# Where the operands of a split-fp32 matmul stream begin in SBUF: 256-byte buffer starts, and four buffers 4 to 28 bytes behind one

## Chip, cores, metric

One NeuronCore of a Trainium2 chip runs the whole program. The metric is the device time of one execution, in microseconds; the median of several runs counts.

## What is computed

A chain of transformer blocks over 512 tokens of 1024 channels, all in float32. `first_block` has two layers, each of a SwiGLU feed-forward, a mixer and a second feed-forward. `second_block` is one layer of two linear recurrences (gated delta rule and mLSTM), an output product, and a product-key expert layer over 16384 experts.

```python
x = x + 0.5 * swiglu(rmsnorm(x, ln_ffn1[l]), w_ffn1_gu[l], w_ffn1_down[l])
z = rmsnorm(x, ln_mix[l]) @ w_in[l]
a = pool_mixer(u_pool, ...) @ w_pool_branch[l]
b = swa_sink_attention(q, k, v, sinks[l]) @ w_attn_branch[l]
x = x + (g_pool * a + g_attn * b) @ w_out[l]
x = x + 0.5 * swiglu(rmsnorm(x, ln_ffn2[l]), w_ffn2_gu[l], w_ffn2_down[l])
...
x = x + concatenate([y_gdn, y_mlstm]) @ w_out_2
x = x + sum over chosen experts of gate * gelu(h . u_e) * v_e
```

## The kernel before

Activations lie transposed, 128 channels on the partitions and 512 tokens along the free dimension, so `x` is [128, 8, 512]. Every large product goes through weight tiles of [128, 2048] float32, 331 of them in all, one after the other through two slots. SP loads a tile into `raw`; ScalarE rounds it to float32r as `w_hi` (`split_hi`, L556); GpSimd writes the rest, `raw - w_hi`, as `w_lo` in four pieces (`low_part`, L448). The moving operand is split in the same way by ScalarE (hi) and VectorE (lo). A product of one 128x128 block is then three float32r matmuls of 512 columns into one PSUM bank (L1161 to L1163):

```python
pe.matmul(out_ap, w_hi[:, slot, cols], m_hi, start=start, stop=False)
pe.matmul(out_ap, w_hi[:, slot, cols], m_lo, start=False, stop=False)
return pe.matmul(out_ap, w_lo[:, slot, cols], m_hi, start=False, stop=stop)
```

The order of all work is written out by hand, engine by engine, with semaphores between them.

The moving operand is `h_hi`/`h_lo` in the gate and up columns, the input columns, the queries and the experts' first products; `act_hi`/`act_lo` ([128, 22, 512]) in the feed-forward's down product (`down`, L1248); `y` and `att` in the mixer's two branch products; `y` again and `mix_late` in its output product; `y2_hi`/`y2_lo` in the second mixer's output product, which the profile also calls y; and `w_mix_hi`/`w_mix_lo` ([128, 2, 4, 512]) in the experts' second products (`v_products`). `act_hi` is written by ScalarE at L590 and `act_lo` by VectorE at L2144; `w_mix_hi` by ScalarE at L1059 and `w_mix_lo` by VectorE at L2818. Groups of four expert rows alternate between two halves of the w_mix buffers.

`place` (L126) gives every buffer its address. It keeps a running offset that it rounds up to 32 bytes after each buffer, and adds `base`, the first free SBUF byte rounded up to 32, which is 16512 here. Buffers that all stages share come first (x, h, raw, w_hi, w_lo, rstd, sq, tmp, then small ones and constants); behind them, from `region`, each stage lays its own buffers over those of the others: the feed-forward, the mixer, the second mixer, the choice of experts, the experts.

Of the kernel before, what the change touches and what calls it, by code (L numbers as in the profile page):

```python
# [20 lines left out]
F32 = mybir.dt.float32  # L21
F32R = mybir.dt.float32r
# [5 lines left out]
P = 128  # L28
TOKENS = 512
# [4 lines left out]
FB = FF // P  # L34
# [8 lines left out]
GH = 4  # L43
# [16 lines left out]
EG = 4  # L60
# [53 lines left out]

GATE_STEP = {"rows": 1, "read": 2, "logs": 3, "a": 4, "sums": 5, "m": 7, "floor": 8}


def build(nc, x_in, weights, gains, small, pool_w, consts, rope, second, level_masks,
          keys, out):
# [2 lines left out]
    with stack:  # L122
        sizes = {F32: 4, F32R: 4, U32: 4}
        offset = [0]

        def place(name, shape, dtype, at=None):  # L126

            nbytes = int(np.prod(shape[1:])) * sizes[dtype]
            if at is None:
                at = offset[0]  # L130
                offset[0] = -(-(at + nbytes) // 32) * 32
            return nc.alloc_sbuf_tensor_at(name, shape, dtype, offset=at + base)

# [8 lines left out]


        x = place("x", [P, KB, TOKENS], F32)
        h_hi = place("h_hi", [P, KB, TOKENS], F32R)
        h_lo = place("h_lo", [P, KB, TOKENS], F32R)
        raw = place("raw", [P, 2, TILE * P], F32)
        w_hi_at = offset[0]
# [8 lines left out]
        rcol = place("rcol", [P, 3, TT], F32)  # L157
        gain = place("gain", [P, 9, KB], F32)
        small_sb = place("small_sb", [P, LAYERS, 14], F32)
        const = place("const", [P, 5, P], F32)  # L160
        mask = place("mask", [P, 2 * P], F32)
        invc = place("invc", [P, 4, PAD], F32)
        headsel = place("headsel", [P, 2], F32)
        rope_sb = place("rope_sb", [P, 2, TOKENS], F32)
        region = offset[0]
        ident, swap, upper, lower, ones = (const[:, n, :] for n in range(5))
# [1 line left out]

        offset[0] = region
        sq_ffn = place("sq_ffn", [P, KB, TOKENS], F32, at=region)  # L170
        act_hi = place("act_hi", [P, FB, TOKENS], F32R)
        act_lo = place("act_lo", [P, FB, TOKENS], F32R)
        gate_s = place("gate_s", [P, TOKENS], F32)
        up_s = place("up_s", [P, TOKENS], F32)
        silu = place("silu", [P, TOKENS], F32)
# [39 lines left out]
        head_gain = place("head_gain", [P, 8], F32)  # L215
        r3 = place("r3", [P, 3, TT, 8], F32)
        rn = place("rn", [P, 3, 32], F32)
        m_row_at = offset[0]
        m_row = place("m_row", [GH, 2, TOKENS], F32)
        head_squares = place("head_squares", [P, GH * P], F32, at=m_row_at)  # L220
        masks2 = place("masks2", [P, 9, P], F32)
        sq_second = place("sq_second", [P, KB, TOKENS], F32, at=offset[0])
# [75 lines left out]
        g_in = place("g_in", [P, 2, CHUNKS, EG, CHUNK], F32)  # L298
        sq_last = place("sq_last", [P, KB, TOKENS], F32, at=offset[0])
        s_in = place("s_in", [P, 2, EG, TOKENS], F32)  # L300
        w_mix_hi = place("w_mix_hi", [P, 2, EG, TOKENS], F32R)
        w_mix_lo = place("w_mix_lo", [P, 2, EG, TOKENS], F32R)
        gelu = place("gelu", [P, TOKENS], F32)
        weighed = place("weighed", [P, 2, TOKENS], F32)

# [2712 lines left out]
```

How the kernel before makes its waits and increments, by code:

```python
    def held(self):  # L89
        self.eng.wait_ge(self.sem, self.value())
# [253 lines left out]
        def wait_delta(eng, r, n):  # L345
            if delta_signals(r) == 7:
                if n < 7:
                    eng.wait_ge(sem("delta_done"), update_base[r] + n + 1)
                else:
                    eng.wait_ge(tile_used, update_end[r])
            elif n % 2 == 0:
                eng.wait_ge(sem("delta_done"), update_base[r] + n // 2 + 1)
            else:
                eng.wait_ge(tile_used, update_end[r] - 4 + n // 2 + 1)
# [64 lines left out]
        @block.sync  # L420
        def _(sp):
            sp.dma_start(raw[:, 0, :], weights[0]).then_inc(tile_landed[0], 16)
            for q in range(X_PARTS):
                sp.dma_start(x[:, 2 * q:2 * q + 2, :], x_in[:, 2 * q:2 * q + 2, :]).then_inc(x_landed[q], 16)
            sp.dma_start(raw[:, 1, :], weights[1]).then_inc(tile_landed[1], 16)
            with sp.Fori(0, (TILES - 2) // 2) as i:
                for slot in range(2):
                    source = sp.snap(2 * i + (2 + slot))
                    sp.wait_ge(lo_written, PIECES * (2 * i + (slot + 1)))
                    sp.dma_start(raw[:, slot, :], weights[source]).then_inc(tile_landed[slot], 16)
            sp.wait_ge(lo_written, PIECES * (TILES - 2))
            sp.dma_start(raw[:, 0, :], weights[TILES - 1]).then_inc(tile_landed[0], 16)
# [32 lines left out]
            def triangle(n, j):  # L466
                pool.wait_ge(sem("decay_exp"), pair_step(n, 1, j))
                e = q_mask[n % 2][j]
```

## Time and profile before

| what | value |
|---|---|
| median of 3 runs | 4127.03 us (4126.63 to 4129.42) |
| the profiled execution's own time | 4125.36 us |
| its span, first to last instruction | 4123.5 us |
| TensorE matmul busy | 4065.8 us, 99% of the span |
| weight loads (beside the matmuls) | 3366.7 us |
| VectorE, GpSimd, ScalarE busy | 1989.2, 1884.4, 1455.7 us |
| granted TensorE clock, mean | 0.997 of full speed |
| DMA | 489.64 MB, 119 GB/s mean |

A matmul's duration in the trace runs from its start until its result is in PSUM, and the next one starts before that; so durations of matmuls overlap, and how fast they follow each other is read from starts or from counts in a stretch. A granted clock of 1.00 is 2.4 GHz.

### The profile page before, as it was taken

Reading aid. Unit: us, or ns where it says so; the run is one execution under the profiler, and the core shown is the slowest. Engines: PE = TensorE matmul, PEld = TensorE weight load, DVE = VectorE, ACT = ScalarE, POOL = GpSimd, SP = SyncE. Lnnn points to the kernel's source line nnn. Section 1 sums busy time; section 2 is a strip of 40 time slices with the busy share of each in tenths; the row PEclk is TensorE's granted clock in tenths of the full one; section 3 lists DMA queues with packets and bytes.
Section 4 is the critical chain, followed back from the end, with each engine's and each line's share of the span. In section 5 each row is a group of like instructions: output and inputs, shape, how many; then the busy total and the mean of one; then the engine's idle time right before and its main releaser. Section 6 shows DMA issues by size and latency. Waiting matters only on the chain.

```text
span 4123.5 us, 52537 instructions
## 1 busy us (share of the span) xinstructions
PE 4065.8 (99%) x19252; PEld 3366.7 (82%) x19252; DVE 1989.2 (48%) x3472; ACT 1455.7 (35%) x2192; POOL 1884.4 (46%) x1408
## 2 busy tenths in 40 slices
PE   8999999999999999999999999999999999999998
PEld 7888777888888877888777998888888888888887
DVE  3212553221320354321148563498788846666653
ACT  3222243222322224322234433333677732222222
POOL 4444334444444434444432644455433345555553
PEclk9999999999999999999999999999999999999999
DMA  3222112222222222222322002233455575555542
GB/s 134 101 99 98 72 72 82 102 94 100 92 97 97 95 72 72 92 93 100 108 72 42 22 22 103 107 138 138 165 205 205 205 248 192 189 198 194 189 166 82
DMA packets 144611, 489.64 MB, mean 119 GB/s; under 512 B 17120, under 2 KB 82912, under 8 KB 101984
## 3 DMA queue, kind: packets, MB, share of 16 engines
q1 hardware_dynamic: 49392, 351.29, 24.2%
q10 hardware_dynamic: 95088, 136.56, 9.7%
q8 instruction: 86, 1.41, 0.1%
q14 instruction: 45, 0.37, 0.0%
HBM read 420.68 MB, written 67.14 MB: 118 GB/s over the span
## 4 chain that ended last, share of the span: by engine, by line
PE 42%; issue 33%; POOL 22%; DVE 2%; ACT 1%; POOLq 0%; ACTq 0%; DVEq 0%
POOL w_lo L448 21%; PE bank L1161 12%; PE bank L1162 12%; PE bank L1163 12%; PE bank L1974 1%; PE bank L1734 1%; PE bank L1750 1%; PE bank L1746 1%; DVE gk L2387 0%; DVE gq L2387 0%; PE bank L1909 0%; POOL b_t L492 0%; DVE p_t L2398 0%; POOL inv_t L484 0%; POOL inv_t L483 0%
## 5 line engine op out<-in xcount | busy, mean ns | idle before, releaser
L448 POOL TENSOR_TENSOR w_lo<-raw,w_hi 128x512 fp32r<-128x512 f32 x1324 | 1781.8, 1377 | 2120.9 <-ACT w_hi L556 2094.2
L1161 PE MATMUL bank<-h_hi,w_hi 128*128 128x512 f32 x3232 | 1270.8, 393 | 21.3 <-DVE h_lo L2101 11.0
L1162 PE MATMUL bank<-h_lo,w_hi 128*128 128x512 f32 x3232 | 1260.0, 390 | 0.0
L1163 PE MATMUL bank<-h_hi,w_lo 128*128 128x512 f32 x3232 | 1259.8, 390 | 0.0
L556 ACT ACTIVATE w_hi<-raw 128x2048 fp32r<-128x2048 f32 x331 | 632.8, 1912 | 1058.7 <-PE bank L1163 1010.0
L1161 PEld LDWEIGHTS bank<-h_hi,w_hi 128*128 128x128 f32 x3232 | 607.7, 188 | 153.0 <-POOL w_lo L448 18.0
L1163 PEld LDWEIGHTS bank<-h_hi,w_lo 128*128 128x128 f32 x3232 | 607.3, 188 | 127.5
L1162 PEld LDWEIGHTS bank<-h_lo,w_hi 128*128 128x128 f32 x3232 | 608.0, 188 | 122.9 <-issue 1.2
L1161 PE MATMUL bank<-w_mix_hi,w_hi 128*128 128x512 f32 x1024 | 398.7, 389 | 0.9 <-ACT stage L964 0.9
L1162 PE MATMUL bank<-w_mix_lo,w_hi 128*128 128x512 f32 x1024 | 398.7, 389 | 0.0
L1163 PE MATMUL bank<-w_mix_hi,w_lo 128*128 128x512 f32 x1024 | 398.7, 389 | 0.0
L2830 DVE TENSOR_TENSOR x<-x,bank 128x512 f32<-128x512 f32 x256 | 172.4, 683 | 246.8 <-PE bank L1163 246.7
L1163 PE MATMUL bank<-act_hi,w_lo 128*128 (+1 forms) x704 | 274.1, 389 | 0.0
L1161 PE MATMUL bank<-act_hi,w_hi 128*128 (+1 forms) x704 | 274.1, 389 | 0.0
L1162 PE MATMUL bank<-act_lo,w_hi 128*128 (+1 forms) x704 | 274.0, 389 | 0.0
L2108 DVE SCALAR_TENSOR_TENSOR x<-bank,x 128x512 f32<-128x512 f32 x56 | 38.1, 681 | 444.4 <-PE bank L1163 444.4
L2140 DVE TENSOR_TENSOR up_s<-bank,rstd 128x512 f32<-128x512 f32 x88 | 60.9, 692 | 383.1 <-PE bank L1163 382.9
L1161 PEld LDWEIGHTS bank<-w_mix_hi,w_hi 128*128 128x128 f32 x1024 | 192.3, 188 | 41.0 <-issue 1.3
L1163 PEld LDWEIGHTS bank<-w_mix_hi,w_lo 128*128 128x128 f32 x1024 | 192.3, 188 | 39.8
L1162 PEld LDWEIGHTS bank<-w_mix_lo,w_hi 128*128 128x128 f32 x1024 | 192.3, 188 | 39.8
L590 ACT ACTIVATE act_hi<-up_s 128x512 f32 (+1 forms) x88 | 55.6, 632 | 460.3 <-DVE up_s L2142 460.3
L989 ACT ACTIVATE hot_parts<-hot_parts,gate_hi 128x128 fp32r<-128x128 f32 x512 | 163.4, 390 | 107.7 <-DVE hot_parts L2771 107.7
(379 smaller groups left out, 4454.3 us busy)
## 6 DMA issues: line engine op xcount, KB each, us to landing
raw<-weights SPq DMA_DIRECT2D x331, 1024.0 KB, 4.8
g_store<-g_buf ACTq DMA_DIRECT2D x8, 4096.0 KB, 18.5
g_in<-g_store ACTq DMA_DIRECT2D x32, 1024.0 KB, 5.5
s_store<-stage ACTq DMA_DIRECT2D x60, 512.0 KB, 2.9
s_in<-s_store ACTq DMA_DIRECT2D x30, 1024.0 KB, 7.5
x<-x_in SPq DMA_DIRECT2D x4, 512.0 KB, 8.0
out<-x SPq DMA_DIRECT2D x8, 256.0 KB, 2.2
q_mask<-rows ACTq DMA_DIRECT2D x6, 256.0 KB, 4.0
```

The lines of the kernel that those rows point to most:

```text
L448: pool.tensor_tensor(w_lo[:, slot, cols], raw[:, slot, cols], w_hi[:, slot, cols].bitcast(F32), ALU.subtract).then_inc(lo_written, 1)
L556: act.activation(w_hi[:, slot, :], raw[:, slot, :], ACT.Copy).then_inc(hi_written, 1)
L590: c_act_hi.up(act.activation(act_hi[:, at, :], prod[:, :], ACT.Copy))
L989: ins = act.activation(part, part.bitcast(F32), ACT.Copy, scale=gate_hi[:, 4 * q + n:4 * q + n + 1].bitcast(F32))
L1161: pe.matmul(out_ap, w_hi[:, slot, cols], m_hi, start=start, stop=False)
L1162: pe.matmul(out_ap, w_hi[:, slot, cols], m_lo, start=False, stop=False)
L1163: return pe.matmul(out_ap, w_lo[:, slot, cols], m_hi, start=False, stop=stop)
L1734: ins = pe.matmul(banks[4 * j][:, h * P:h * P + P], b_t[j][:, h, :], inv[j][:, h, :], start=True, stop=True)
L1746: ins = pe.matmul(banks[b + 1][:, h * P:h * P + P], t[:, h, :], prod_y[j][:, h, :], start=True, stop=True)
L1750: ins = pe.matmul(banks[b + 2][:, h * P:h * P + P], prod_y[j][:, h, :], t[:, h, :], start=True, stop=True)
L2140: c_us.step(dve.tensor_tensor(up_s[:, :], banks[up_bank][:, :], rstd[:, :], ALU.mult))
L2830: c_x.up(dve.tensor_tensor(x[:, d, :], x[:, d, :], banks[4 + d % 4][:, :], ALU.add))
```

## The change

`place` rounds the start of a buffer of 2048 bytes or more up to a multiple of 256, counted from the same base, instead of 32. `m_row`, whose place is written out, is rounded in the same way. A new function `place_behind` allocates a buffer with `lead` extra float32 columns in front and hands out the part behind them; it is used for `act_hi` (4 columns, 16 bytes), `act_lo` (2 columns, 8 bytes), `w_mix_hi` (1 column, 4 bytes) and `w_mix_lo` (7 columns, 28 bytes). `headsel`, 8 bytes long, moves ahead of the constants. No instruction is added or removed, and none changes its engine, shape or order.

```diff
+LINE = 256
+        def place_behind(lead, name, shape, dtype):
+
+            count = int(np.prod(shape[1:]))
+            whole = place(name, [P, lead + count], dtype)
+            part = whole[:, lead:lead + count]
+            if len(shape) == 3:
+                return part.rearrange("p (a t) -> p a t", a=shape[1])
+            return part.rearrange("p (a b t) -> p a b t", a=shape[1], b=shape[2])
+
         def place(name, shape, dtype, at=None):
 
             nbytes = int(np.prod(shape[1:])) * sizes[dtype]
             if at is None:
-                at = offset[0]
+                step = LINE if nbytes >= 2048 else 32
+                at = -(-offset[0] // step) * step
                 offset[0] = -(-(at + nbytes) // 32) * 32
             return nc.alloc_sbuf_tensor_at(name, shape, dtype, offset=at + base)
...
+        headsel = place("headsel", [P, 2], F32)
         const = place("const", [P, 5, P], F32)
         mask = place("mask", [P, 2 * P], F32)
         invc = place("invc", [P, 4, PAD], F32)
-        headsel = place("headsel", [P, 2], F32)
...
-        act_hi = place("act_hi", [P, FB, TOKENS], F32R)
-        act_lo = place("act_lo", [P, FB, TOKENS], F32R)
+        act_hi = place_behind(4, "act_hi", [P, FB, TOKENS], F32R)
+        act_lo = place_behind(2, "act_lo", [P, FB, TOKENS], F32R)
...
-        m_row_at = offset[0]
-        m_row = place("m_row", [GH, 2, TOKENS], F32)
+        m_row_at = -(-offset[0] // LINE) * LINE
+        m_row = place("m_row", [GH, 2, TOKENS], F32, at=m_row_at)
+        offset[0] = m_row_at + 2 * TOKENS * 4
...
-        w_mix_hi = place("w_mix_hi", [P, 2, EG, TOKENS], F32R)
-        w_mix_lo = place("w_mix_lo", [P, 2, EG, TOKENS], F32R)
+        w_mix_hi = place_behind(1, "w_mix_hi", [P, 2, EG, TOKENS], F32R)
+        w_mix_lo = place_behind(7, "w_mix_lo", [P, 2, EG, TOKENS], F32R)
```

## Rows read from the trace of the kernel before

**Rows 1.** The page's head: span, then busy time, share and instructions by engine.

```profile
span 4123.5 us, 52537 instructions
PE 4065.8 (99%) x19252; PEld 3366.7 (82%) x19252; DVE 1989.2 (48%) x3472; ACT 1455.7 (35%) x2192; POOL 1884.4 (46%) x1408
```

**Rows 2.** TensorE's groups by line and shape: count, busy us, mean ns of one.

```profile
L1162 PE MATMUL bank<-w_mix_lo,w_hi 128*128 128x512 f32 x1024 | 398.7, 389 | 0.0
...
L1162 PE MATMUL bank<-act_lo,w_hi 128*128 x512 | 199.3, 389 | 0.0
...
L1162 PE MATMUL bank<-y_lo,w_hi 128*128 128x512 f32 x192 | 77.0, 401 | 0.0
...
L1162 PE MATMUL bank<-act_lo,w_hi 128*128 128x512 f32 x192 | 74.7, 389 | 0.0
...
L1162 PE MATMUL bank<-att_lo,w_hi 128*128 128x512 f32 x64 | 25.3, 395 | 0.0
...
L1162 PE MATMUL bank<-mix_late,w_hi 128*128 128x512 f32 x64 | 25.3, 395 | 0.0
...
L1372 PE MATMUL bank<-pool_s,v_tok 128*64 128x512 f32 x28 | 13.7, 607 | 0.0
```

**Rows 3.** TensorE by stretch (act, h, w_mix, y, att, y2): length, busy (count), clock, DMA.

```profile
262.00:374.00 112.00, 112.00 (x496) 1.00 0.27 95
80.00:240.00 160.00, 160.00 (x708) 1.00 0.28 98
3440.00:3560.00 120.00, 120.00 (x531) 1.00 0.54 191
572.50:593.50 21.00, 21.00 (x92) 1.00 0.19 65
595.00:616.00 21.00, 21.00 (x92) 1.00 0.18 62
2503.00:2545.00 42.00, 42.00 (x182) 1.00 0.24 79
```

**Rows 4.** Timeline of TensorE in the att branch product: start us, duration us.

```profile
600.21 0.40 PE L1163 MATMUL bank<-att_hi,w_lo 128*128 128x512 f32 x1
600.45 0.39 PE L1161 MATMUL bank<-att_hi,w_hi 128*128 128x512 f32 x1
600.67 0.40 PE L1162 MATMUL bank<-att_lo,w_hi 128*128 128x512 f32 x1
600.91 0.39 PE L1163 MATMUL bank<-att_hi,w_lo 128*128 128x512 f32 x1
```

**Rows 5.** Timeline of TensorE: an h column that starts after other work.

```profile
2230.15 0.40 PE L1162 MATMUL bank<-h_lo,w_hi 128*128 128x512 f32 x1
...
2232.01 0.39 PE L1161 MATMUL bank<-h_hi,w_hi 128*128 128x512 f32 x1
...
2234.28 0.39 PE L1162 MATMUL bank<-h_lo,w_hi 128*128 128x512 f32 x1
```

**Rows 6.** Operands' writers: timeline of VectorE, ScalarE; then act_lo's instructions (min/median/max ns).

```profile
2138.72 3.12 DVE L2387 SCALAR_TENSOR_TENSOR gq<-conv_in,conv_sb,gq 128x512 f32<-128x512 f32 x4
2141.87 1.42 DVE L2426 COPY mv<-bank 128x512 f32<-128x512 f32 x2
...
3516.75 1.53 DVE L2818 TENSOR_TENSOR w_mix_lo<-weighed,w_mix_hi 128x512 fp32r<-128x512 f32 x1
...
3521.58 1.92 ACT L556 ACTIVATE w_hi<-raw 128x2048 fp32r<-128x2048 f32 x1 [8.44 <-PE bank L1163]
...
L2144 DVE TENSOR_TENSOR act_lo<-up_s,act_hi x88: 691/693/694, 36.0 to 1923.0; 128x512 f32 x80, 128x512 fp32r<-128x512 f32 x8
...
  ACT act_hi L590: 85.9, 88
```

**Rows 7.** Whom TensorE waited for, longest first.

```profile
PE bank L1161 <- POOL w_lo L448: 14.5, 10, 2.3
```

**Rows 8.** Timeline of TensorE: four full-f32 matmuls of 512 columns.

```profile
545.85 1.93 PE L1372 MATMUL bank<-pool_s,v_tok 128*64 128x512 f32 x4
```

## The prediction

> **What bounds the kernel now.** The page comes first, and on it the share of busy time [rows 1]: TensorE (PE) is busy for 4065.8 of 4123.5 us, and no other engine passes 1990. Next the groups by shape [rows 2]: the lines of the split product (L1161 to L1163, of which only L1162 is shown) make nearly all of it, each a 128x512 matmul. Their durations (389 to 401 ns) overlap, so they can't be added; what counts is the pitch, from one start to the next. Third, then, the stretches with their matmul counts [rows 3]: the count holds the matmul running at either edge, so the pitch is length over count less 2, and the granted clock is 1.00 in all of them, the 2.4 GHz level. Fourth, the timeline for single starts [rows 4, 5]. Last, what TensorE waited for [rows 7]: its longest entry, the low halves of the weight tiles, is 14.5 us in all. So a change reaches the end in one of two ways: it changes the pitch, or it makes some feeder late by more than its slack.
>
> **What the pitch shows.** 512 columns at 2.4 GHz are 213.3 ns. With act_hi/act_lo as the moving operand it is 112/494 = 226.7 ns, with h 160/706 = 226.6, with w_mix 120/529 = 226.8 [rows 3]. With y and att in the branch products it is 21/90 = 233.3, and with the second mixer's y, in the output product, 42/180 = 233.3 [rows 3]. Same helper, same shape, same stationary tiles, same clock, and 6.7 ns apart.
>
> What separates them is the place of the moving operand against the weights. `place` puts each buffer at the next multiple of 32, from a base of 16512, which is 128 past a multiple of 256. Adding up the sizes in the code, w_hi and w_lo start 128 past a multiple of 256, and so do h, act and w_mix. The buffers of the mixing stage from qk on (att, y, mix_late too) start at 0, since pool_s before them is 4224 bytes, and y2 starts at 96. So the pitch is 226.7 where operand and weights agree modulo 256, and 233.3 where they differ by 128 or by 32. The timeline says the same in another way: after an idle time an h product starts as slowly as a y product (2230.15 to 2232.01 is 8 pitches, 232.5 ns each) and then settles (2232.01 to 2234.28 is 10, 227 each) [rows 5]. In the att products starts 0.24 and 0.22 us apart alternate without end [rows 4]. That reads as a rhythm between two address streams, the weight load of the next matmul and the moving operand of this one, with a quiet state that only some offsets can hold. It is read from coincidence in one trace and not shown.
>
> **The change, part by part.** *1. All large buffers at multiples of 256 from the same base.* From x to tmp nothing moves. `headsel` goes ahead of `const`, which then falls on a multiple by itself, and the region behind `rope_sb` starts where it did. In the mixing stage, the buffers from qk on move by 128 and agree with the weights; in the second mixer those from m_row on move from 96 to 128. If the reading above holds, all products with y, att, mix_late and y2 fall to 226.7: 3 x (192 + 64 + 64) = 960 matmuls [rows 2]. Some 30 of them stand at waits or pay an idle start, which leaves 930, and I take 6.5 ns each instead of 6.7 for those that aren't in the slow rhythm throughout: 6.0 us. TensorE paces all three stretches without a gap, so the end gets it. If the reading is false this part is worth 0. The other buffers that move feed matmuls of full f32, and VectorE, ScalarE and GpSimd instructions. VectorE reads conv_in at taps 4 to 16 bytes apart in 3.12 us for four, 0.78 each, and writes mv, whose rows are 520 bytes long and so fall 8 bytes further each time, in 1.42 us for two [rows 6]. An aligned act_lo takes 0.693 [rows 6]. So an address off its line costs VectorE at most 0.1 us, and these moves 0.
>
> *2. act_hi, act_lo, w_mix_hi and w_mix_lo begin 16, 8, 4 and 28 bytes further.* First the writers. ScalarE writes the hi parts, VectorE the lo parts. VectorE sat idle 85.9 us before 88 act_lo writes, and one FFN step of 48 matmuls lasts 10.9 us. For w_mix the last lo write of a group, at 3516.75, ends at 3518.28. The group before is done at 3521.58, where ScalarE takes up its last weight tile [rows 6]; its last matmul began 0.39 earlier and the next group's first follows one pitch on, at 3521.4, so there are 3.1 us of slack against four writes. A doubled write (0.69 more) would still be hidden. I take 0; without that cover it would be 128 x 0.69 = 88 us.
>
> Then the reader, which is on the path. 3 x 1024 + 3 x (512 + 192) = 5184 matmuls stream a shifted operand [rows 2]. The trace has no split product at such an offset. The nearest row is y2's, 32 bytes off the weights' phase and at 233.3. Bounds: from below, all of the 13.3 ns over the 213.3 go (5184 x 13.3 = 69 us faster); from above, each matmul falls to the slow rhythm (5184 x 6.67 = 34.6 us slower). I take 0, because what the shifted operands keep is the block they begin in: 4 to 28 bytes past 128 modulo 256 is still within the weights' own 32, while both slow cases begin in another one. That the fast pitch is a settled state, reached again after each disturbance [rows 5], speaks for its bearing a shift of a few columns. The place where I chose is here, and it carries nearly all the risk.
>
> The Trainium skill ("SBUF — State Buffer", Door 1: The DMA port swizzle, its note on cachelines) says that SBUF has lines of 16 bytes and that crossing to a new one costs something. A 2048-byte operand at 4, 8 or 28 bytes touches 129 of them instead of 128, at 16 bytes still 128. No run here shows the price of a line.
>
> *The sum:* -6.0 + 0 + 0 = -6.0 us. The profiled execution took 4125.36 us beside a span of 4123.5; against its own time the sum gives 4119.4. The median of the runs is 4127.03, and I forecast 4127.0 - 6.0 = **4121.0 us**, with 4117 to 4125 as this case's own range. I count 0.2%, 8.3 us, as what a measurement can tell from no change, and this case lies inside it.
>
> **The rivals.**
>
> *A, the shifted operands lose the settled state (ends slower).* All 5184 matmuls run at 233.3: +34.6 - 6.0 = +28.6, 4155.6 us. For it: the 32 bytes of y2 were enough, and nothing in the trace shows a tolerance. Against it: both slow cases begin in another 32-byte block than the weights. It decides as soon as more than (6.0 + 8.3)/6.67 ns = some 2150 of the 5184 are slow, so FFN alone (2112) or w_mix alone (3072) sits near or past the point.
> *B, a partial line or column pair costs a little on each.* Between 0 and A, say 1 to 3 ns: 5184 x 1 to 3 = 5 to 16 us, 4126 to 4137.
> *C, the shift takes operand and weights out of each other's way.* The pitch falls toward 213.3: 3 ns to all 13.3, 4105 down to 4052 us. For it: the 13.3 ns are there in each quiet stretch, and it isn't work. Against it: three different phases and hundreds of unsettled starts gave no stretch under 226.6.
> *D, placement doesn't matter and the change does nothing.* y and att are slow for another reason: 4127 us. The phases of 0 and 96 agree on exactly 233.3, which speaks a little for it; that h starts slow and recovers speaks against. The skill ("TensorE: Matmul & The Clock Gate", Part 2, LDWEIGHTS) holds that the two read ports are independent and that a weight load takes no read bandwidth from the running matmul; by that, D. The trace doesn't fit it well, as two pitches of one shape stand side by side [rows 3].
> *E, an odd multiple of 4 bytes halves the rate.* w_mix_hi (4) and w_mix_lo (28) can't be cut in pairs of columns. The price is that of a full f32 matmul of 512 columns: four in 1.93 us, the last 0.607 long [rows 2, 8], so (1.93 - 0.607)/3 = 0.44 us each, and 3072 x (0.44 - 0.227) = +654 us, about 4775. No buffer here is read by TensorE from an odd multiple of 4, so nothing excludes it.
>
> **How the numbers follow.** My forecast 0.42, A 0.20, B 0.13, C 0.12, D 0.08, E 0.05. The range 4113 to 4157 leaves out C and E, and holds the rest but for its edges, some 8 in 10. Faster by over 0.2%: C and the lower edge of my case, 0.18. Slower: A, E and the upper half of B, 0.31. Within: 0.51.
>
> **What would show it.** In the new trace: the branch and output products at 226.7 (92 to 94 matmuls in 21 us, h's density) would bear out part 1; act and w_mix still at 496 matmuls in 112 us and 531 in 120 bear out part 2's zero; 482 and 516 say A; more than 500 and 536 say C; w_mix near 273 says E. Act_lo and w_mix_lo should keep their durations, and the waits for POOL's w_lo their 14.5 us. My forecast is wrong above all if the tolerance of the settled state is finer than 4 to 28 bytes.

## The result: 0.7% slower

The changed kernel takes 4157.90 us (4154.47 to 4158.77, 4 runs), the kernel before 4128.17 in its 4 runs beside it: ratio 1.0072, interval 1.0058 to 1.0086. The profiled execution took 4158.65 us beside a span of 4156.9, so the two spans are 33.4 us apart. Both parts of the change are in the time, with opposite signs (experiments 2 and 3). Two executions, one of the kernel before at 10596 us and one in experiment 5 at 12467 us, were far slower than all others and are left out of the ratios; the median of 4121.18 given there counts its one and is 4120.58 without it.

The head of the page after, for [rows 1]. TensorE's matmul time has grown by 32.5 us, that of its weight loads by 6.4, and no other engine's has moved by more than 3.

```profile
span 4156.9 us, 52617 instructions
PE 4098.3 (99%) x19252; PEld 3373.1 (81%) x19252; DVE 1986.3 (48%) x3472; ACT 1455.8 (35%) x2192; POOL 1885.3 (45%) x1408
```

TensorE's stretches after, for [rows 3]: act, h, w_mix, att, y2, each in the place that its product now has. The columns are length, busy (count), clock, DMA share, GB/s.

```profile
262.00:374.00 112.00, 112.00 (x482) 1.00 0.26 94
80.00:240.00 160.00, 160.00 (x708) 1.00 0.28 98
3440.00:3560.00 120.00, 120.00 (x516) 1.00 0.50 179
597.00:618.00 21.00, 21.00 (x94) 1.00 0.25 82
2515.50:2557.50 42.00, 42.00 (x186) 1.00 0.23 79
```

Read by length over count less 2: act has gone from 226.7 to 112/480 = 233.3 ns, w_mix from 226.8 to 120/514 = 233.5, h is where it was, and att and y2 have gone from 233.3 to about 228 (21/92 and 42/184, where one matmul more or less is 1%).

The timeline after tells att more exactly, for [rows 4]. In att the starts are now 0.22 or 0.23 us apart, 0.68 for three; the alternation is gone.

```profile
600.20 0.39 PE L1174 MATMUL bank<-att_hi,w_hi 128*128 128x512 f32 x1
600.42 0.39 PE L1175 MATMUL bank<-att_lo,w_hi 128*128 128x512 f32 x1
600.65 0.39 PE L1176 MATMUL bank<-att_hi,w_lo 128*128 128x512 f32 x1
600.88 0.39 PE L1174 MATMUL bank<-att_hi,w_hi 128*128 128x512 f32 x1
```

The feeders kept out of it: the wait of [rows 7], then the writers of the shifted operands (act_lo for [rows 6]; w_mix_lo's median was 1002 ns before).

```profile
PE bank L1174 <- POOL w_lo L461: 13.9, 10, 2.4
...
L2157 DVE TENSOR_TENSOR act_lo<-up_s,act_hi x88: 692/693/695, 36.0 to 1929.6; 128x512 f32 x80, 128x512 fp32r<-128x512 f32 x8
...
L2831 DVE TENSOR_TENSOR w_mix_lo<-weighed,w_mix_hi x128: 677/1000/1783, 3373.6 to 4102.1; 128x512 fp32r<-128x512 f32 x128
```

### The profile page after: what moved, and what is told of

Read it like the earlier page. It is cut to its first block, busy times and chain, and to the rows that moved or that the text cites. A ratio compares the mean times of both kernels' runs of the same rounds, so it can differ in the third digit from the quotient of the medians.

```text
span 4156.9 us, 52617 instructions
## 1 busy us (share of the span) xinstructions
PE 4098.3 (99%) x19252; PEld 3373.1 (81%) x19252; DVE 1986.3 (48%) x3472; ACT 1455.8 (35%) x2192; POOL 1885.3 (45%) x1408
## 4 chain that ended last, share of the span: by engine, by line
PE 43%; issue 33%; POOL 22%; DVE 2%; ACT 1%; POOLq 0%; ACTq 0%; DVEq 0%
POOL w_lo L461 21%; PE bank L1174 12%; PE bank L1176 12%; PE bank L1175 12%; PE bank L1987 1%; PE bank L1747 1%; PE bank L1763 1%; PE bank L1759 1%; DVE gk L2400 0%; DVE gq L2400 0%; PE bank L1922 0%; POOL b_t L505 0%; DVE p_t L2411 0%; POOL inv_t L497 0%; POOL inv_t L496 0%
## 5 line engine op out<-in xcount | busy, mean ns | idle before, releaser
L1174 PE MATMUL bank<-w_mix_hi,w_hi 128*128 128x512 f32 x1024 | 408.2, 399 | 0.9 <-ACT stage L977 0.9
```

## Experiments

**1. TensorE alone.** The first question was what a shift costs and what it is measured against. This kernel streams 144 split matmuls (6 times 8 blocks of 3) for each of 41 settings, each setting to one PSUM bank, and leaves the transformer out. The shifts (hi, lo of the moving operand; hi, lo of the weights) are in bytes from 128 past a multiple of 256.

```diff
+SAME = (0, 4, 8, 12, 16, 20, 24, 28, 32, 40, 48, 64, 80, 96, 112, 128, 144, 160, 176, 192, 208, 224, 240, 252)
+CONFIGS = [(m, m, 0, 0) for m in SAME]
+CONFIGS += [(0, 0, 0, 0)]
+CONFIGS += [(4, 4, 4, 4), (16, 16, 16, 16), (32, 32, 32, 32), (128, 128, 128, 128), (0, 0, 128, 128), (0, 0, 32, 32),
+            (0, 0, 16, 16)]
+CONFIGS += [(16, 8, 0, 0), (4, 28, 0, 0), (4, 0, 0, 0), (0, 4, 0, 0), (16, 0, 0, 0), (0, 16, 0, 0), (0, 128, 0, 0),
+            (0, 0, 0, 128)]
+CONFIGS += [(0, 0, 0, 0)]
...
+                for r in range(REPEAT):
+                    bank = banks[k % 8]
+                    for n in range(BLOCKS):
+                        blk = (2 * n + r % 2) * P
+                        for part, (w, m) in enumerate(((0, 0), (0, 1), (1, 0))):
+                            ins = pe.matmul(bank[:, :], ww[w][:, blk:blk + P], mm[m][:, n, :],
+                                            start=n == 0 and part == 0, stop=n == BLOCKS - 1 and part == 2)
```

> Only TensorE streams: 41 settings of 144 split-fp32 matmuls (128x128 weights, 512 columns) each, back to back; each setting shifts the moving operand (hi, lo) and the weights (hi, lo) by so many bytes from 128 past a multiple of 256. The transformer is left out. Theory 1, what counts is the moving operand's place against the weights: 226.7 ns per matmul at a difference of 0, also where both are shifted alike by 4, 16, 32 or 128; 233.3 or more for operand shifts of 128 and of 224 (as y and y2 in the kernel before), for (16, 8) 233.3 and for (4, 28) about 234 (as act and w_mix in the kernel after), and a tolerance, if there is one, of under 4 bytes. Theory 2, the operand's own address counts: operands unshifted give 226.7 whatever the weights do (so weights shifted by 128, 32 or 16 alone stay at 226.7), and all shifted by 128 give 233.3. Theory 3, it is hi and lo that must agree with each other: (16, 16) and (4, 4) give 226.7, (16, 8) and (4, 28) more.

The timeline of TensorE in this run has one row for each setting, in the order of the list; from one row's start to the next, divided by 144, is the setting's pitch. Here stand those of (4, 4), (8, 8), (12, 12); (16, 16), (20, 20), (24, 24); (240, 240), (252, 252); (4, 4, 4, 4), (16, 16, 16, 16), (32, 32, 32, 32), (128, 128, 128, 128), (0, 0, 128, 128), (0, 0, 32, 32).

```profile
57.38 34.43 PE L91 MATMUL bank_b<-mv,wt 128*128 128x512 f32 x144
91.65 33.77 PE L91 MATMUL bank_c<-mv,wt 128*128 128x512 f32 x144
125.26 33.13 PE L91 MATMUL bank_d<-mv,wt 128*128 128x512 f32 x144
158.23 33.51 PE L91 MATMUL bank_e<-mv,wt 128*128 128x512 f32 x144
191.58 34.67 PE L91 MATMUL bank_f<-mv,wt 128*128 128x512 f32 x144
226.09 33.90 PE L91 MATMUL bank_g<-mv,wt 128*128 128x512 f32 x144
...
762.50 32.81 PE L91 MATMUL bank_g<-mv,wt 128*128 128x512 f32 x144
795.14 33.37 PE L91 MATMUL bank_h<-mv,wt 128*128 128x512 f32 x144
...
861.01 34.40 PE L91 MATMUL bank_b<-mv,wt 128*128 128x512 f32 x144
895.25 33.44 PE L91 MATMUL bank_c<-mv,wt 128*128 128x512 f32 x144
928.52 32.80 PE L91 MATMUL bank_d<-mv,wt 128*128 128x512 f32 x144
961.16 32.85 PE L91 MATMUL bank_e<-mv,wt 128*128 128x512 f32 x144
993.85 33.76 PE L91 MATMUL bank_f<-mv,wt 128*128 128x512 f32 x144
1027.44 33.77 PE L91 MATMUL bank_g<-mv,wt 128*128 128x512 f32 x144
1061.05 33.76 PE L91 MATMUL bank_h<-mv,wt 128*128 128x512 f32 x144
```

So with a shift of 4 bytes the pitch is (91.65 - 57.38)/144 = 238.0 ns, 8 bytes 233.4, 12 bytes 229.0, 16 bytes (191.58 - 158.23)/144 = 231.6, 20 bytes (226.09 - 191.58)/144 = 239.7. All with the weights together: by 32 and by 128 226.7 and 227.0, but by 4 237.8 and by 16 231.0. Weights alone by 128 233.3, by 32 233.4. From rows not shown: weights alone by 16 gave 233.3, and the moving hi or lo alone by 4, 16 or 128 gave 231.1 to 235.5. Of the 24 equal shifts of hi and lo, 240 gave 226.7 and 0, entered again further on (its first row holds the start at the lower clock), 226.8; all others gave at least 228.6; 128 gave 232.4, 224 gave 233.3; (16, 8) gave 233.3 and (4, 28) 233.4, which are the leads of act and w_mix, and the pitches that they have in the changed kernel.

Theory 2 falls (weights alone moved by 128 slow it, all moved by 128 don't), and theory 3 (16 and 16, 4 and 4 agree with each other and are slow). Theory 1 holds for the steps of 32 and 128 bytes that were tried and not for 4 and 16, where moving weights and operand together doesn't help. The quiet 240 is outside it and is taken up in experiments 8 and 9. There is no tolerance of 4 bytes.

**2. and 3. Each part alone.** In the changed kernel, first the leads at 0, then `step = 32` and `LINE = 32`.

```diff
-        act_hi = place_behind(4, "act_hi", [P, FB, TOKENS], F32R)
+        act_hi = place_behind(0, "act_hi", [P, FB, TOKENS], F32R)
...
-                step = LINE if nbytes >= 2048 else 32
+                step = 32
```

> The changed kernel with the four leads set to 0, so all large buffers at multiples of 256 and nothing behind them. By the prediction's part 1: the y, att, mix_late and y2 products at 226.7 ns and the time 6 us under the kernel before, 4122 us, ratio 0.9985. If the shift of the buffers costs somewhere else (the changed kernel's h products have some 3 us more in sum), 4125.

> The four leads alone, all else rounded to 32 as before. Rival A by the pitches of the changed kernel: FFN 2112 matmuls x 6.7 = 14 us and w_mix 3072 x 7.5 = 23 us, so 37 us over the kernel before, 4165 us, ratio 1.009; y, att and mix_late lie behind nothing of this and stay at 233.3. If the two parts interact (one shifts the other's phase), anything else between 4150 and 4170.

Alignment alone: 4123.20 us against 4127.48, ratio 0.9990, interval 0.9981 to 0.9999. Leads alone: 4166.81 us, ratio 1.0097, interval 1.0082 to 1.0113. Both are near what was expected, and 0.9990 x 1.0097 = 1.0087 is the change's 1.0072 within the intervals. The second kernel's leads are not quite those of the change, though. With every buffer rounded to 32, `act_lo` and `w_mix_lo` follow a hi buffer that its lead has made longer, and come to lie 40 and 60 bytes past the weights' place instead of 8 and 28 (by the sizes in the code). Its w_mix stretch stands at 120/511 = 234.8 ns, where the changed kernel has 233.5: some 4 of the 39 us belong to that. The line of the leads alone:

```profile
3480.00:3600.00 120.00, 120.00 (x513) 1.00 0.53 190
```

In the aligned kernel's stretches act and w_mix are as before, and y2 at 42/185 = 227.0:

```profile
262.00:374.00 112.00, 112.00 (x495) 1.00 0.27 95
3440.00:3560.00 120.00, 120.00 (x531) 1.00 0.52 184
2500.50:2542.50 42.00, 42.00 (x187) 1.00 0.22 80
```

**4. and 5. Who is measured against whom, in the whole kernel.** From the aligned kernel without leads: `offset[0] += 128` ahead of `w_hi`; and, in another, the base 128 further.

```diff
+        offset[0] += 128
         w_hi_at = offset[0]
...
-        base = -(-base // 32) * 32
+        base = -(-base // 32) * 32 + 128
```

> The kernel with aligned buffers and no leads, but w_hi and w_lo 128 bytes further (all others still 128 past a multiple of 256). Relative place (theory 1): all 15864 split matmuls of 512 columns at 233.3 ns instead of 226.7, so up to 15864 x 6.67 = 106 us over the aligned kernel's 4123, less what stands at waits: 4220 to 4229 us. Theory 2, the operand's own address: no operand moves, so 4123 us. h, act and w_mix, which make nine tenths of it, would show it in the trace.

> The kernel with aligned buffers and no leads, its base 128 bytes further, so that weights and operands alike begin at multiples of 256. Theory 1: nothing changes, 226.7 ns everywhere and 4123 us. Theory 2: all at 233.3, some 4229 us.

Weights alone moved: 4202.34 us against 4125.32, ratio 1.0186 (1.0169 to 1.0203). All moved: 4121.18 us, ratio 0.9988 (0.9978 to 0.9998), the aligned kernel's time. The first is slower, but by 79 us over the aligned kernel and not 97 or more. Its stretches (act, w_mix) say why in part, with 112/482 = 232.4 and 120/516 = 232.6 ns where 233.3 was expected; at 232.4, 15864 matmuls would still give some 90 us. The rest was not traced to its matmuls.

```profile
262.00:374.00 112.00, 112.00 (x484) 1.00 0.27 99
3480.00:3600.00 120.00, 120.00 (x518) 1.00 0.52 184
```

A difference of 128 bytes thus has more than one slow pitch: 232.4 was also what experiment 1 gave for operands moved by 128, and 233.3 for weights moved by 128.

**6. Fewer weight columns, shorter rows, drawn shifts.** The stream of experiment 1 with other settings, again without the transformer.

```diff
+CONFIGS = [(0, 0, 0, 0, m, TOKENS) for m in (128, 128, 96, 64, 32)]
+CONFIGS += [(128, 128, 0, 0, m, TOKENS) for m in (128, 64, 32)]
+CONFIGS += [(4, 4, 0, 0, m, TOKENS) for m in (128, 64, 32)]
+CONFIGS += [(m, m, 0, 0, P, 256) for m in (0, 128, 4)]
+CONFIGS += [(0, 0, w, w, P, TOKENS) for w in (4, 8, 12, 20, 24, 28, 48, 64, 240)]
+CONFIGS += [(m, m, 0, 0, P, TOKENS) for m in (248, 244, 236, 232, 228, 216)]
+CONFIGS += [(240, 0, 0, 0, P, TOKENS), (0, 240, 0, 0, P, TOKENS), (0, 0, 0, 16, P, TOKENS), (0, 0, 0, 240, P, TOKENS)]
...
+                            ins = pe.matmul(bank[0:cols, 0:width], ww[w][:, blk:blk + cols], mm[m][:, n, 0:width],
```

> TensorE alone again, 144 matmuls per setting, the transformer left out. The 13.3 ns over the 213.3 of 512 columns are either taken by the weight load (theory L: they shrink with the number of weight columns, 6.7 ns at 64 and 3.3 at 32, and so does what a shift of 128 or 4 adds, and with 256 moving columns they stay 13.3), or belong to the moving stream (theory M: they don't depend on weight columns, and halve with 256 moving columns). Weights shifted by 4 to 28 bytes against an unshifted operand: 229 to 240 ns by the first such run. Twelve drawn combinations of shifts by multiples of 16: none under 226.7 if that is the floor of the pattern; one of them under it would be worth a kernel.

The timeline, unshifted operands: weight columns 128, 96, 64, 32 and the row behind them; then 256 moving columns at 0, 128 and 4 and the row behind them; last the low weights alone shifted by 16 and by 240 and the row behind them.

```profile
56.77 32.80 PE L96 MATMUL bank_b<-mv,wt 128*128 128x512 f32 x144
89.41 33.29 PE L96 MATMUL bank_c<-mv,wt 128*96 128x512 f32 x144
122.53 33.28 PE L96 MATMUL bank_d<-mv,wt 128*64 128x512 f32 x144
155.65 33.52 PE L96 MATMUL bank_e<-mv,wt 128*32 128x512 f32 x144
189.01 33.62 PE L96 MATMUL bank_f<-mv,wt 128*128 128x512 f32 x144
...
391.51 17.43 PE L96 MATMUL bank_d<-mv,wt 128*128 128x256 f32 x144
408.78 17.26 PE L96 MATMUL bank_e<-mv,wt 128*128 128x256 f32 x144
425.87 17.90 PE L96 MATMUL bank_f<-mv,wt 128*128 128x256 f32 x144
443.61 33.62 PE L96 MATMUL bank_g<-mv,wt 128*128 128x512 f32 x144
...
1012.57 32.80 PE L96 MATMUL bank_h<-mv,wt 128*128 128x512 f32 x144
1045.21 32.80 PE L96 MATMUL bank_a<-mv,wt 128*128 128x512 f32 x144
1077.85 33.60 PE L96 MATMUL bank_b<-mv,wt 128*128 128x512 f32 x144
```

226.7, 230.0, 230.0 and 231.7 ns: fewer weight columns make it slower. Half the moving columns give 119.9 at 0, which is 106.7 and again 13.3, then 118.7 at 128 and 123.2 at 4. Both theories of the 13.3 ns fall: L, as they don't shrink with the weight columns but grow; M, as they don't halve with the moving ones. They are a cost per matmul, whose source stays open.

What a shift of 128 adds is another matter. It is there with 128 weight columns and 512 moving ones (232.4 against 226.7). With 64 and 32 weight columns it is gone (229.3 and 230.7, from rows not shown, against 230.0 and 231.7), and with 256 moving columns the shifted stream is 1.2 ns faster than the unshifted one. A shift of 4 is slow in all of them (237.8 and 238.3 with 64 and 32 weight columns). That a difference of 128 costs something is thus shown for the shape of this kernel and for no other.

Both weights shifted by 4 to 28 bytes gave 229.9 to 234.9. The low weights alone by 16 and by 240 gave 226.7 both times, so the two weights don't have to agree to the byte; by 128 (in experiment 1) they gave 231.2. Of the twelve drawn combinations none was under 226.7, nor was any other setting of 512 columns, unless by the last digit of a row; the lowest of the twelve was 228.8.

**7. and 8. Other leads in the whole kernel.** The aligned kernel with all four leads at 5 columns, and at 60.

```diff
-        act_hi = place_behind(0, "act_hi", [P, FB, TOKENS], F32R)
+        act_hi = place_behind(5, "act_hi", [P, FB, TOKENS], F32R)
```

> Aligned buffers, and act_hi, act_lo, w_mix_hi and w_mix_lo all 20 bytes behind. If the pitch of the stream-only runs carries over (240.0 ns at 20 and 20), act and w_mix stand at 240 and the time is 5184 x 13.3 = 69 us over the aligned kernel's 4122: 4191 us. If only the fact of a shift counts, not its size (the theory that any lead ends in the 233.3 state), 4122 + 35 = 4157 us, as with the leads of the change.

> The same with all four 240 bytes behind (16 before the next multiple of 256). The stream-only run had 226.67 ns at 240 and 240, as at 0: act and w_mix at 226.7 and 4122 us, the aligned kernel's time, 35 us under the changed one. If a lead of any size costs, 4157 us or more.

20 bytes: 4188.85 us, ratio 1.0150 (1.0133 to 1.0166), 2 us from what the stream's pitch foretold, and act stands at 112/467 = 239.8, w_mix at 120/499 = 240.5:

```profile
262.00:374.00 112.00, 112.00 (x469) 1.00 0.26 94
...
3480.00:3600.00 120.00, 120.00 (x501) 1.00 0.51 184
```

240 bytes: 4165.44 us, ratio 1.0085 (1.0068 to 1.0102). The stream had foretold 4122, and that was wrong: act is at 112/480 = 233.3 and w_mix at 120/507 = 236.7. A pitch of the stream thus carried over at 20 bytes and not at 240.

```profile
262.00:374.00 112.00, 112.00 (x482) 1.00 0.26 94
...
3480.00:3600.00 120.00, 120.00 (x509) 1.00 0.51 184
```

**9. Why 240 was quiet once.** The stream again, without the transformer, with 240 entered after different settings, with higher address bits changed, and in the orders of the down product and of the expert rows.

```diff
+CONFIGS = [c + ("column",) for c in (
+    (0, 0, 0, 0), (0, 0, 0, 0), (240, 240, 0, 0), (20, 20, 0, 0), (240, 240, 0, 0), (224, 224, 0, 0), (240, 240, 0, 0),
+    (240, 496, 0, 0), (240, 240, 0, 256), (496, 496, 0, 0), (496, 240, 0, 256), (0, 256, 0, 0), (0, 0, 0, 256),
+    (256, 256, 0, 0), (20, 20, 0, 0), (0, 0, 0, 0))]
+CONFIGS += [c + ("down",) for c in ((0, 0, 0, 0), (240, 240, 0, 0), ..., (16, 8, 0, 0), (128, 128, 0, 0))]
+CONFIGS += [c + ("rows",) for c in ((0, 0, 0, 0), (240, 240, 0, 0), ..., (4, 28, 0, 0), (4, 284, 0, 0), (128, 128, 0, 0))]
```

> TensorE alone, 144 matmuls per setting, the transformer left out. It asks why a lead of 240 bytes was quiet in the first such run (226.67 ns) and not in the kernel (233.3 for act, 236.4 for w_mix). Theory H, the state depends on what ran before: 240 after 0, after 20 and after 224 gives different pitches in the column order. Theory O, it depends on the order in which blocks and rows follow: the column order stays at 226.67 at 240, the orders of the down product (two rows in turn) and of the expert rows (four in turn) don't. Theory B, a higher address bit counts: with lo or the low weights 256 bytes further the pitch at 240 changes. In all three a shift of 0 stays at 226.67, also when all operands move by 256, and (16, 8) and (4, 28) give 233.3 in the kernel's own orders.

The third to seventh settings and the row behind: 240, 20, 240, 224, 240, and 240 with 496.

```profile
90.65 33.76 PE L101 MATMUL bank_c<-mv,wt 128*128 128x512 f32 x144
124.25 34.68 PE L101 MATMUL bank_d<-mv,wt 128*128 128x512 f32 x144
158.77 34.24 PE L101 MATMUL bank_e<-mv,wt 128*128 128x512 f32 x144
192.84 33.75 PE L101 MATMUL bank_f<-mv,wt 128*128 128x512 f32 x144
226.44 33.76 PE L101 MATMUL bank_g<-mv,wt 128*128 128x512 f32 x144
260.04 33.76 PE L101 MATMUL bank_h<-mv,wt 128*128 128x512 f32 x144
```

After 0, 240 runs at (124.25 - 90.65)/144 = 233.3, after 20 at (192.84 - 158.77)/144 = 236.6, after 224 at 233.3, where experiment 1 had 226.7 after 224. So the same addresses have two steady pitches, 233.3 and 236.6, which are about those of experiment 8, and what ran before picks one: theory H, for these two. The orders give the same 233.3 (theory O falls), and so do 256 bytes more on lo, on the low weights, on hi and lo together, or on hi and the low weights (theory B falls as far as it was tried).

The quiet 226.7 at 240 did not come back, and why it came once stays open. The two streams differ in their earlier settings, but also in their buffers: in experiment 1 the lo operand and the low weights both lay an odd multiple of 256 bytes behind the hi operand, and here both lie an even multiple behind it (`SPAN` is 16896 instead of 16640, `WSPAN` 8704 instead of 8448). Here each was moved by 256, but never both with hi and the high weights in place, so a higher address bit is as possible a cause as earlier work.

Shift 0 is different in kind: it came out at 226.7 to 226.9 in each of its settings here but the first, which begins with a dozen matmuls 0.43 us apart, the 1.2 GHz level, after 20 as after 240, and with 256 added to lo, to the low weights or to all. (16, 8) in the down order and (4, 28) in the order of the rows gave 233.3 and 233.4.

## Why the prediction was wrong, point by point

- **What bounds the kernel** held: the span grew by 33.4 us, TensorE's busy time by 32.5, and no feeder's grew by more than 1.
- **The reading of the pitch**, that operand and weights are measured against each other modulo 256, held for this shape in the steps of 32 and 128 bytes that were tried, and not below. It was read from coincidence; experiments 4 and 5 show it in the whole kernel (weights moved alone: 1.0186; all moved: 0.9988) and experiment 1 in the stream.
- **Part 1, all large buffers at multiples of 256**, held in mechanism: att went to three starts in 0.68 us, 226.7 each, and y2 to 227.0 in experiment 2. The term was -6.0 us; alone it measured 4127.48 to 4123.20, -4.3 us, interval -0.4 to -7.8, which holds the -6.0. The other moved buffers cost nothing that can be seen.
- **Part 2, the writers at 0**, held: act_lo 693 ns as before, w_mix_lo's median 1000 beside 1002, and TensorE's wait for weights 13.9 us beside 14.5.
- **Part 2, the reader at 0, is the step that failed.** The text said that "what the shifted operands keep is the block they begin in: 4 to 28 bytes past 128 modulo 256 is still within the weights' own 32", and that a settled state would bear "a shift of a few columns". Neither is so. Within those 32 bytes the stream gave 238.0, 233.4, 229.0, 231.6 and 239.7 at 4, 8, 12, 16 and 20 bytes, and only 0 is quiet. The measured price is the text's own upper bound: act 2112 x (233.3 - 226.7) = 14 us, w_mix 3072 x (233.5 - 226.8) = 21 us, together 35 us where 34.6 stood as the bound and 0 was taken. The leads alone measured +39 us, some 4 of them from the lo operands' other places in experiment 3.
- **The wrong inference** was from "recovers from a disturbance in time" to "bears a disturbance in address". [Rows 5] show the first. They say nothing of the second; and the one row with a small offset that there was, y2 at 32 bytes, was slow. By that row, which the text called the nearest, rival A was the forecast: 4155.6 us, beside 4157.9 measured.
- **Rival A** is what happened, in its place, price and point of decision: FFN and w_mix are both past it. B, C and D are excluded by the act and w_mix stretches (482 and 516, the numbers given for A). E too: leads of 4 and 28 bytes ran at 233.5, not 440.
- **The range**, 4113 to 4157, ended 1.4 us above A's own figure and so left no room for what A was uncertain by; the measured 4157.9 lies outside it.
- **Left over:** 14 + 21 - 5 for the products of part 1 is 30, and the two spans are 33.4 us apart. The difference is clock, as far as it can be read. TensorE's mean granted clock was 0.995 in the profiled execution after and 0.997 in the one before. Of the 70 us from 2085, in the second mixer's input products, it was 0.93 after and 1.00 before, with 8 matmuls fewer; first after, then before:

```profile
2085.00:2155.00 70.00, 66.98 (x297) 0.93 0.41 91
```

```profile
2085.00:2155.00 70.00, 67.03 (x305) 1.00 0.33 76
```

  Timed executions of equal mean clock are 29 to 31 us apart. At 0.997 there is one after at 4154.47 us, beside 4123.35 to 4125.32 of the kernel before in all its runs; at 0.995 there are 4158.65 and 4158.77, beside 4128.93 to 4129.66. Why the clock differs from one execution to the next, no run tried.

Alignment alone, with either base, is the best version of those tried, 0.1% under the kernel before; no lead that was tried helps.

## What to carry to other kernels

Where a kernel is bound by back-to-back float32r matmuls, compare the pitches of its products with one another before looking for waits; two pitches for one shape can come from placement. Put moving operands and weights at the same offset modulo 256, on a multiple of 32: with 128 weight columns and 512 moving ones nothing that was tried beat that here, while 20 bytes off cost 1.5%. For other shapes measure it, as with 256 moving columns a difference of 128 bytes was 1% faster. And take the pitch from the whole kernel before relying on it: the lead of 240 bytes, quiet in one stream, came out at a ratio of 1.0085 there. And where a cost must be bounded by its nearest row, take that row's value unless a row, not an argument, speaks for another.

## What the runs showed of the hardware

- A split matmul of 512 float32r columns, 213.3 ns of streaming at 2.4 GHz, ran at a pitch of 226.7 ns at best in all runs and at up to some 240 (20 bytes off: 239.7 in the stream, 239.8 for act in the kernel). With 256 columns the unshifted extra was 13.3 ns too. It grew when the weights had fewer columns (230.0 at 64, 231.7 at 32).
- The extra depends on the addresses. At 128 weight columns and 512 moving ones it left the pitch at 226.7 to 227.0 in every setting in which operand and weights agree modulo 256 and begin at 0, 128 or 160 modulo 256 (experiments 1, 5, 6 and 9, but for the first matmuls of each run at the lower clock). All at 4 bytes past 128, in agreement, ran at 237.8. Elsewhere the stream was that quick in two cases: the low weights alone off by 16 or 240, and once both operands off by 240.
- A difference of 128 bytes cost 5.7 to 6.6 ns with 128 weight columns and 512 moving ones. With 64 or 32 weight columns, or 256 moving ones, it cost nothing (the stream of experiment 6, one setting of each).
- Off the quiet place the same addresses can have more than one steady pitch (233.3 and 236.6 at 240 bytes in experiment 9), and earlier work picks one. The timed runs of experiment 8 lie from 4154 to 4167 us; that this is the reason was not tried.
- The Trainium skill ("TensorE: Matmul & The Clock Gate", Part 2, LDWEIGHTS) says that weight loads take no read bandwidth from a running matmul. Moving the weights alone made the whole kernel 1.9% slower, so for float32r the two are not independent in time; by what path, no run here shows.
